# An accumulating gather for the first expert row of each token, in the combine stage of a mixer and mixture-of-experts block

## The chip, the cores and the metric

The kernel runs on one core of a Trainium2 chip. The metric is the device time of one execution in microseconds (us), and lower is better. The engines of the core are named as the profile names them: PE (matrix multiplications; PEld is its weight load), DVE (vector), ACT (scalar, activations), POOL (general purpose, and issuer of indirect DMAs) and SP (issuer of plain DMAs). Each works through its own list in order and is held only by semaphores. Sixteen DMA engines move the data of all DMAs.

## What is computed

One block of a diffusion transformer over 512 tokens of width 1024, in float32: a parallel mixer (short convolution, multiscale pooling, neighbourhood attention, Fourier mix), then a mixture of experts in which each token goes to 2 of 16 experts, then a last norm. The part that the change touches is the end:

```python
def moe_ffn(h, router_w, router_b, w1, w3, w2):
    ...
    _, idx = lax.top_k(masked, TOP_K)                      # two experts for each token
    ...
    for e in range(N_EXPERTS):
        he = jax.nn.silu(h @ w1[e]) * (h @ w3[e])
        y = y + gates[:, e:e + 1] * (he @ w2[e]).astype(F32)
    return y.astype(h.dtype)
...
    f = moe_ffn(tokens, ...)
    x = x + g2 * f[:b * n].reshape(b, n, d)
    ...
return rms_norm(x, final_g)
```

So each output row is the residual row plus two scaled expert rows, divided by its root mean square and multiplied by `final_g`.

## The kernel before, in words

The mixer and the routing come first, then the experts. Each expert has a block of up to 128 token rows (and there are spare blocks for experts that are chosen by more). The blocks run in pairs, one after the other: the matrix products stand on PE, the splits of each float32 weight into a high and a low part on ACT and DVE. A block ends in `ysb`, 128 rows of 1024 values that are already multiplied by gate and `g2`, and ACT stores them in a table in device memory, `expert_rows` (`y_dram` in the code).

The combine stage begins while the last block is still on PE. It works on four chunks of 128 tokens, t = 0 to 3. `x1[:, t, :]` holds the residual rows, `slot_idx[:, t, k]` says in which row of the table the k-th expert row of a token stands, and two banks of PSUM (`tok_bank(t, half)`, 512 columns each) hold the sum of chunk t. The last block of all is not read back from the table: `y_hi` and `y_lo`, its rows split in two, are multiplied by a 0/1 matrix `last_hot` on PE and land in the same banks (`last_to_tokens`). Four steps surround the change:

- POOL (L801 to L808) waits until the rows of all blocks but the last are in the table, and issues eight gathers, two for each chunk, into `ygat[:, t, 0, :]` and `ygat[:, t, 1, :]`. Both gathers of a chunk raise `gat_in[t]` by 16.
- DVE adds, for the chunks 0, 1 and 2, the first gathered row to the residual (`add_first`, L2207, which waits for `gat_in[t]`) and then the second gathered row to that, into PSUM (`add_second`, L2211, which raises `xsum_ok`). Between the ones for chunk 0 and the others stand the scaling of the last block's rows (L2138) and the low half of its split (L2217).
- For chunk 3, ACT copies the residual into PSUM (L1705, raises `x3_ok`), and PE adds both gathered rows by multiplying them with the identity (`gathered_row`, L1325).
- When PE has finished chunk t (`tok_ok`), ACT squares and sums it (L1709) and takes a root (L1712), DVE takes the reciprocal (L2221) and scales both halves (`result`, L2224), and SP stores each half in `out` (L634). Each of these runs over t = 0 to 3 in this order on its engine.

The order on every engine is written out by hand. A semaphore `fresh_ok` says that the PSUM banks of a chunk have been opened by a matrix product (L1290).

Of the kernel before, what the change touches and what calls it, by code (L numbers as in the profile page):

```python
# [30 lines left out]
ALU = mybir.AluOpType  # L31
# [40 lines left out]
def build(nc, x, c, ctx, c_ctx, ada_w, ada_b, norm1_g, norm2_g, w_in, conv_w, pool_w, pool_scale,  # L72
# [3 lines left out]
    y_dram = nc.dram_tensor("expert_rows", ((NB + 1) * P, D), F32, kind="Internal").ap()  # L76
# [4 lines left out]
    with stack:  # L81
        def at(name, offset, shape, dt=F32):
            return nc.alloc_sbuf_tensor_at(name, shape, dt, offset=base + int(offset))

        def sem(name):
            return stack.enter_context(nc.semaphore(name))
# [47 lines left out]
        ygat = at("ygat", 0, [P, NT, 2, D])  # L134
# [7 lines left out]
        x1 = at("x1", 128 * K1, [P, NT, D])  # L142
# [40 lines left out]
        def small(name, shape, dt=F32, pool=1):  # L183
            n = int(np.prod(shape[1:])) * mybir.dt.size(dt)
            n = (n + 31) // 32 * 32
            t = at(name, cursor[pool], shape, dt)
            cursor[pool] += n
            return t

        ident = small("ident", [P, P])  # L190
# [25 lines left out]
        slot_idx = small("slot_idx", [P, NT, 2], I32)  # L216
# [56 lines left out]
        psum = stack.enter_context(nc.psum_tensor("psum", [P, 8, 512], F32))  # L273
# [136 lines left out]
        gat_in = [sem(f"gat_in{i}") for i in range(NT)]  # L410
        xsum_ok = sem("xsum_ok")
        x3_ok = sem("x3_ok")
        fresh_ok = sem("fresh_ok")
        ylast_hi_ok = sem("ylast_hi_ok")
        ylast_lo_ok = sem("ylast_lo_ok")
        tok_ok = sem("tok_ok")
# [38 lines left out]
        def tok_bank(t, half):  # L455

            return bank[2 * t + half]
# [183 lines left out]
        def _(gp):  # L641
# [160 lines left out]
            gp.wait_ge(ysb_free[1], n_pairs * 16)  # L802
            gp.sem_inc(gather_go, 1)
            for t in range(NT):
                for k in range(2):
                    gp.indirect_dma_start(ygat[:, t, k, :], None, y_dram,
                                          bass.IndirectOffsetOnAxis(ap=slot_idx[:, t, k:k + 1], axis=0)
                                          ).then_inc(gat_in[t], 16)  # L808

# [2 lines left out]
        def _(pe):  # L814
# [198 lines left out]
            for h in range(2):  # L1013
                pe.matmul(bank[4 + h][:], pw[:, h, :], dpool[:, h, :],
                          start=True, stop=True).then_inc(pool_ps, 1)

            for t in range(NT):
                for h in range(2):
                    m = pe.matmul(bank[t][:, h * GW:(h + 1) * GW], fT[:, h, t * P:(t + 1) * P], head_dft[:],
                                  start=True, stop=True)  # L1020
# [130 lines left out]
            for i in range(NT):  # L1151
                m = pe.matmul(bank[7][:, NT * NE:(NT + 1) * NE], ones_b[:], sel[:, i, :],
                              start=(i == 0), stop=(i == NT - 1))
# [3 lines left out]
            for i in range(2 * NT):  # L1157
                m = pe.matmul(bank[6][:, 0:2 * NE], hot_slot[:, i, :], hot_base[:, i].rearrange("p a b -> p (a b)"),
                              start=(i == 0), stop=(i == 2 * NT - 1))
# [160 lines left out]
            pe.wait_ge(y1_copied, last + 1)  # L1320
            whole_bank_written(6).then_inc(fresh_ok, 1)

            def gathered_row(half, k):
                hs = slice(half * 512, (half + 1) * 512)
                return pe.matmul(tok_bank(3, half)[:], ident[:], ygat[:, 3, k, hs], start=False, stop=(k == 1))  # L1325

            def last_to_tokens(t, half):
                hs = slice(half * 512, (half + 1) * 512)
                cols_ = last_hot[:, t * P:(t + 1) * P]
                pe.wait_ge(ylast_hi_ok, half + 1)  # L1330
                pe.matmul(tok_bank(t, half)[:], cols_, y_hi[:, hs], start=False, stop=False)
                pe.wait_ge(ylast_lo_ok, half + 1)
                return pe.matmul(tok_bank(t, half)[:], cols_, y_lo[:, hs], start=False, stop=(t < 3))

            pe.wait_ge(xsum_ok, 1)
            last_to_tokens(0, 0)
            last_to_tokens(0, 1).then_inc(tok_ok, 1)
            pe.wait_ge(x3_ok, 1)
            for half in range(2):
                last_to_tokens(3, half)  # L1340
            pe.wait_ge(xsum_ok, 2)
            last_to_tokens(1, 0)
            last_to_tokens(1, 1).then_inc(tok_ok, 1)
            pe.wait_ge(gat_in[3], 32)
            for half in range(2):
                gathered_row(half, 0)
            pe.wait_ge(xsum_ok, 3)
            last_to_tokens(2, 0)
            last_to_tokens(2, 1).then_inc(tok_ok, 1)
            gathered_row(0, 1)  # L1350
            gathered_row(1, 1).then_inc(tok_ok, 1)

# [2 lines left out]
        def _(act):  # L1357
# [342 lines left out]
            for half in range(2):  # L1700
                hs = slice(half * 512, (half + 1) * 512)
                act.wait_ge((y0_copied, y1_copied)[half], last + 1)
                act.copy(y_hi[:, hs], ysb[1][:, hs]).then_inc(ylast_hi_ok, 1)
            act.wait_ge(fresh_ok, 4)
            act.copy(psum[:, 6:8, :].rearrange("p a n -> p (a n)"), x1[:, 3, :]).then_inc(x3_ok, 1)  # L1705

            for t in range(NT):
                act.wait_ge(tok_ok, t + 1)
                act.activation(ygat[:, t, 0, :], psum[:, 2 * t:2 * t + 2, :].rearrange("p a n -> p (a n)"), ACT.Square,  # L1709
                               accum_out=st2[:, t, 6:7]).then_inc(ss3_ok, 1)  # L1710
                act.wait_ge(ss3_ok, t + 1)
                act.activation(st2[:, t, 7:8], st2[:, t, 6:7], ACT.Sqrt, bias=eps[:], scale=1.0 / D  # L1712
                               ).then_inc(root3_ok, 1)

# [2 lines left out]
        def _(v):  # L1719
            step = [0]  # L1720

            def link(ins):

                step[0] += 1
                ins.then_inc(dve_step, 1)
                v.wait_ge(dve_step, step[0])
# [59 lines left out]
            for n in range(4, 10):  # L1786
                a = ADA_SLOT[n]
# [331 lines left out]
            def low_hidden(b, s):  # L2119
                v.wait_ge(het_hi_ok, s + 1)  # L2120
                v.tensor_tensor(heT_lo[b][:].rearrange("p k t -> p (k t)"), bank[4],
                                heT_hi[b][:].rearrange("p k t -> p (k t)"), ALU.subtract).then_inc(het_lo_ok, 1)
# [8 lines left out]
            def expert_rows(b, s, i, half):  # L2131

                v.wait_ge((y0_ok, y1_ok)[half], s + 1)
                if half == 0:
                    v.wait_ge(ysb_free[b], i * 16 + 16)
                    v.wait_ge(gs_ok, s + 1)
                cs_ = slice(half * 512, (half + 1) * 512)
                v.scalar_tensor_tensor(out=ysb[b][:, cs_], in0=bank[5 + half], scalar=gs1[b][:, 0:1],  # L2138
                                       in1=rows[:, G2, cs_], op0=ALU.mult, op1=ALU.mult
                                       ).then_inc((y0_copied, y1_copied)[half], 1)  # L2140
# [61 lines left out]
            final = n_pairs - 1  # L2202
            block_(0, last - 1, last - 2, n_pairs - 2, last - 3)

            def add_first(t):
                v.wait_ge(gat_in[t], 32)
                link(v.tensor_tensor(x1[:, t, :], ygat[:, t, 0, :], x1[:, t, :], ALU.add))  # L2207

            def add_second(t):
                v.wait_ge(fresh_ok, t + 1)  # L2210
                v.tensor_tensor(psum[:, 2 * t:2 * t + 2, :].rearrange("p a n -> p (a n)"), ygat[:, t, 1, :], x1[:, t, :],  # L2211
                                ALU.add).then_inc(xsum_ok, 1)
# [30 lines left out]
            v.tensor_scalar(last_hot[:], iota_tok[:], idx_last[:, 0:1], None, ALU.is_equal).then_inc(hot_ok, 1)  # L2243
            gated(last)
            low_hidden(1, last)
            add_first(0)
            expert_rows(1, last, final, 0)
            add_second(0)
            expert_rows(1, last, None, 1)
            low_last(0)  # L2250
            low_last(1)
            for t in (1, 2):
                add_first(t)
                add_second(t)
            v.wait_ge(gain_in, 48)
            for t in range(NT):
# [45 lines left out]
```

## Time and profile before

| | before |
|---|---|
| median of 3 runs | 601.15 us |
| lowest and highest of these | 600.04 and 601.83 us |
| profiled execution, its own time | 599.58 us |
| its span, first to last instruction | 597.8 us |
| granted TensorE clock, mean over the span | 0.977 of full |

The span is 1.8 us shorter than the time of the same execution. PE is busy for 553.1 us of the span, DVE for 442.8, ACT for 320.3 and POOL for 155.7. These shares are averages over stages with different limits; what is touched here lies in the last 30 us, from the first gather at 569.5 us to the end of the last store.

### The profile page before, as it was taken

Reading aid. Unit: us, or ns where it says so; the run is one execution under the profiler, and the core shown is the slowest. Engines: PE = TensorE matmul, PEld = TensorE weight load, DVE = VectorE, ACT = ScalarE, POOL = GpSimd, SP = SyncE. Lnnn points to the kernel's source line nnn. Section 1 sums busy time; section 2 is a strip of 40 time slices with the busy share of each in tenths; the row PEclk is TensorE's granted clock in tenths of the full one; section 3 lists DMA queues with packets and bytes.
Section 4 is the critical chain, followed back from the end, with each engine's and each line's share of the span. In section 5 each row is a group of like instructions: output and inputs, shape, how many; then the busy total and the mean of one; then the engine's idle time right before and its main releaser. Section 6 shows DMA issues by size and latency. Waiting matters only on the chain.

```text
span 597.8 us, 7516 instructions
## 1 busy us (share of the span) xinstructions
PE 553.1 (93%) x2681; PEld 412.6 (69%) x2681; DVE 442.8 (74%) x569; ACT 320.3 (54%) x394; POOL 155.7 (26%) x139
## 2 busy tenths in 40 slices
PE   1789998999999999985998999999999999999995
PEld 1345873677676787752577887888888888778772
DVE  1358693545586545428769999999999999999868
ACT  4530133345424922235438766768766768766624
POOL 5000916333220700023243113333112333110060
PEclk9789999999999999987999999999999999999998
DMA  8999997369223720058769999999999999999665
GB/s 309 389 371 321 379 369 254 101 191 357 72 70 128 247 84 36 35 210 303 241 227 390 365 398 391 392 392 392 389 392 391 390 392 390 370 383 369 209 213 210
DMA packets 89323, 172.05 MB, mean 288 GB/s; under 512 B 5514, under 2 KB 19022, under 8 KB 89298
## 3 DMA queue, kind: packets, MB, share of 16 engines
q1 hardware_dynamic: 83010, 153.34, 71.7%
q10 hardware_dynamic: 2768, 9.97, 4.1%
q0 software_dynamic: 3520, 8.42, 4.0%
q8 instruction: 15, 0.25, 0.2%
q14 instruction: 10, 0.07, 0.0%
HBM read 158.58 MB, written 17.32 MB: 294 GB/s over the span
## 4 chain that ended last, share of the span: by engine, by line
PE 76%; DMA 10%; DVE 5%; SPq 4%; ACT 3%; issue 1%; DVEq 0%; ACTq 0%; POOLq 0%
DMA ada<-in_ada_w 9%; PE psum L1209 5%; PE psum L1210 5%; PE psum L1211 5%; PE psum L1221 5%; PE psum L1220 5%; PE psum L1219 5%; PE psum L1236 4%; PE psum L1238 4%; PE psum L1237 4%; PE psum L934 3%; PE psum L936 3%; PE psum L935 3%; PE psum L1071 2%; PE psum L1183 2%; PE psum L1073 2%
## 5 line engine op out<-in xcount | busy, mean ns | idle before, releaser
L2116 DVE TENSOR_TENSOR w_lo<-w,w_hi 128x2048 fp32r<-128x2048 f32 x32 | 72.9, 2280 | 2.4 <-ACT w_hi L1622 2.4
L2105 DVE TENSOR_TENSOR w_lo<-w,w_hi 128x1024 fp32r<-128x1024 f32 (+2 forms) x30 | 68.7, 2293 | 0.0
L1622 ACT CAST w_hi<-w 128x2048 fp32r<-128x2048 f32 x32 | 60.3, 1918 | 10.7 <-DMA w<-in_moe_w 5.2
L1613 ACT CAST w_hi<-w 128x2048 fp32r<-128x2048 f32 x30 | 57.2, 1910 | 14.8 <-PE psum L1221 10.9
L2099 DVE TENSOR_TENSOR w_lo<-w,w_hi_a 128x2048 fp32r<-128x2048 f32 (+1 forms) x30 | 51.5, 1755 | 3.0 <-ACT w_hi_a L1609 2.7
L763 POOL COPY idx<-idx 128x1 int32 (+1 forms) x14 | 11.7, 833 | 153.0 <-PE psum L1183 152.4
L1236 PE MATMUL psum<-w_hi,heT_hi 128*128 128x512 f32 x120 | 49.7, 414 | 0.7 <-DVE w_lo L2116 0.7
L1238 PE MATMUL psum<-w_hi,heT_lo 128*128 128x512 f32 x120 | 47.0, 392 | 0.0
L1210 PE MATMUL psum<-w_lo,xgT_hi 128*128 128x512 f32 x120 | 46.8, 390 | 0.0
L1237 PE MATMUL psum<-w_lo,heT_hi 128*128 128x512 f32 x120 | 46.7, 389 | 0.0
L1219 PE MATMUL psum<-w_hi,xgT_hi 128*128 128x512 f32 x120 | 46.7, 389 | 0.0
L1220 PE MATMUL psum<-w_lo,xgT_hi 128*128 128x512 f32 x120 | 46.7, 389 | 0.0
L1221 PE MATMUL psum<-w_hi,xgT_lo 128*128 128x512 f32 x120 | 46.7, 389 | 0.0
L1609 ACT CAST w_hi_a<-w 128x1024 fp32r<-128x1024 f32 x45 | 44.2, 1049 | 0.6 <-DMA w<-in_moe_w 0.6
L1791 DVE SCALAR_TENSOR_TENSOR rows<-ada,cc,rows 128x512 f32<-128x512 f32 x48 | 37.9, 792 | 7.6 <-DMA ada<-in_ada_w 6.1
L780 POOL COPY gs<-gslot 128x1 f32 x14 | 34.4, 2457 | 30.1 <-DVE ysb L2138 30.1
L704 POOL TENSOR_TENSOR win_lo<-win,win_hi 128x1024 fp32r<-128x1024 f32 x10 | 23.8, 2385 | 61.8 <-ACT win_hi L1407 61.8
L1645 ACT ACTIVATE sg<-psum 128x512 f32<-128x512 f32 x16 | 9.6, 599 | 56.1 <-PE psum L1211 50.2
L934 PE MATMUL psum<-hT_hi,win_hi 128*128 128x512 f32 x80 | 33.1, 414 | 3.5 <-DVE z L1859 1.5
L1209 PE MATMUL psum<-w_hi_a,xgT_hi 128*128 128x512 f32 x90 | 36.2, 402 | 0.1
L1211 PE MATMUL psum<-w_hi_a,xgT_lo 128*128 128x512 f32 x90 | 35.1, 390 | 0.0
L936 PE MATMUL psum<-hT_hi,win_lo 128*128 128x512 f32 x80 | 31.3, 392 | 0.0
(345 smaller groups left out, 1255.0 us busy)
## 6 DMA issues: line engine op xcount, KB each, us to landing
w<-in_moe_w SPq DMA_DIRECT2D x32, 2048.0 KB, 14.3
w<-in_moe_w SPq DMA_DIRECT2D x32, 1024.0 KB, 14.0
ada<-in_ada_w SPq DMA_DIRECT2D x12, 2048.0 KB, 18.1
win<-in_w_in SPq DMA_DIRECT2D x8, 1024.0 KB, 14.1
expert_rows<-ysb ACTq DMA_DIRECT2D x15, 512.0 KB, 6.3
expert_rows<-zero SPq DMA_DIRECT2D x1, 5120.0 KB, 21.3
wout<-in_w_out SPq DMA_DIRECT2D x4, 1024.0 KB, 4.9
x<-in_x SPq DMA_DIRECT2D x2, 1024.0 KB, 9.9
```

The lines of the kernel that those rows point to most:

```text
L1209: pe.matmul(bank[2][:], xgT_hi[:, k, :], w_hi, start=(k == 0), stop=False)
L1210: pe.matmul(bank[2][:], xgT_hi[:, k, :], w1_lo[b][:, k, :], start=False, stop=False)
L1211: m = pe.matmul(bank[2][:], xgT_lo[:, k, :], w_hi, start=False, stop=(k == KD - 1))
L1219: pe.matmul(bank[3][:], xgT_hi[:, k, :], w3_hi[:, k, :], start=(k == 0), stop=False)
L1220: pe.matmul(bank[3][:], xgT_hi[:, k, :], w3_lo[b][:, k, :], start=False, stop=False)
L1221: m = pe.matmul(bank[3][:], xgT_lo[:, k, :], w3_hi[:, k, :], start=False, stop=(k == KD - 1))
L1236: pe.matmul(bank[5 + half][:], heT_hi[b][:, k, :], w2_hi[:, k, hs], start=(k == 0), stop=False)
L1237: pe.matmul(bank[5 + half][:], heT_hi[b][:, k, :], w2_lo[b][:, k, hs], start=False, stop=False)
L1238: m = pe.matmul(bank[5 + half][:], heT_lo[b][:, k, :], w2_hi[:, k, hs], start=False, stop=(k == KF - 1))
L1622: act.copy(w2_hi[:, :, hs], w2_sb[b][:, :, hs]).then_inc(w2_hi_ok[half], 1)
L2105: v.tensor_tensor(w3_lo[b][:, ks, :], w3_sb[b][:, ks, :], w3_hi[:, ks, :], ALU.subtract).then_inc(w3_lo_ok, n)
L2116: v.tensor_tensor(w2_lo[b][:, :, hs], w2_sb[b][:, :, hs], w2_hi[:, :, hs], ALU.subtract).then_inc(w2_lo_ok[half], 1)
```

## The change

The first gather of each chunk adds its rows to `x1[:, t, :]` while it moves them; the second gather stays as it was. `add_first` goes away on DVE, and `add_second` now waits for `gat_in[t]`. On PE, chunk 3 takes only one gathered row, and it comes after the chunks 1 and 2. On ACT, the copy of `x1[:, 3, :]` into PSUM waits for `gat_in[3]` and stands behind the square and the root of chunk 0.

```diff
@@ gpsimd @@
             for t in range(NT):
-                for k in range(2):
-                    gp.indirect_dma_start(ygat[:, t, k, :], None, y_dram,
-                                          bass.IndirectOffsetOnAxis(ap=slot_idx[:, t, k:k + 1], axis=0)
-                                          ).then_inc(gat_in[t], 16)
+                gp.indirect_dma_start(x1[:, t, :], None, y_dram,
+                                      bass.IndirectOffsetOnAxis(ap=slot_idx[:, t, 0:1], axis=0),
+                                      compute_op=ALU.add).then_inc(gat_in[t], 16)
+                gp.indirect_dma_start(ygat[:, t, 1, :], None, y_dram,
+                                      bass.IndirectOffsetOnAxis(ap=slot_idx[:, t, 1:2], axis=0)
+                                      ).then_inc(gat_in[t], 16)
@@ tensor @@
             last_to_tokens(0, 1).then_inc(tok_ok, 1)
+            pe.wait_ge(xsum_ok, 2)
+            last_to_tokens(1, 0)
+            last_to_tokens(1, 1).then_inc(tok_ok, 1)
+            pe.wait_ge(xsum_ok, 3)
+            last_to_tokens(2, 0)
+            last_to_tokens(2, 1).then_inc(tok_ok, 1)
             pe.wait_ge(x3_ok, 1)
             for half in range(2):
                 last_to_tokens(3, half)
-            pe.wait_ge(xsum_ok, 2)
-            last_to_tokens(1, 0)
-            last_to_tokens(1, 1).then_inc(tok_ok, 1)
-            pe.wait_ge(gat_in[3], 32)
-            for half in range(2):
-                gathered_row(half, 0)
-            pe.wait_ge(xsum_ok, 3)
-            last_to_tokens(2, 0)
-            last_to_tokens(2, 1).then_inc(tok_ok, 1)
-            gathered_row(0, 1)
-            gathered_row(1, 1).then_inc(tok_ok, 1)
+            gathered_row(0)
+            gathered_row(1).then_inc(tok_ok, 1)
@@ scalar @@
-            act.wait_ge(fresh_ok, 4)
-            act.copy(psum[:, 6:8, :].rearrange("p a n -> p (a n)"), x1[:, 3, :]).then_inc(x3_ok, 1)
 
             for t in range(NT):
...
                 act.activation(st2[:, t, 7:8], st2[:, t, 6:7], ACT.Sqrt, bias=eps[:], scale=1.0 / D
                                ).then_inc(root3_ok, 1)
+                if t == 0:
+                    act.wait_ge(gat_in[3], 32)
+                    act.wait_ge(fresh_ok, 4)
+                    act.copy(psum[:, 6:8, :].rearrange("p a n -> p (a n)"), x1[:, 3, :]).then_inc(x3_ok, 1)
@@ vector @@
-            def add_first(t):
+            def add_second(t):
                 v.wait_ge(gat_in[t], 32)
-                link(v.tensor_tensor(x1[:, t, :], ygat[:, t, 0, :], x1[:, t, :], ALU.add))
-
-            def add_second(t):
                 v.wait_ge(fresh_ok, t + 1)
...
-            add_first(0)
             expert_rows(1, last, final, 0)
             add_second(0)
...
             for t in (1, 2):
-                add_first(t)
                 add_second(t)
```

How this moves instructions is shown in two places. On ACT at the end, before (`x_111` is `x1`; `st_173` holds the sums and roots):

```order
L1703 CAST y_hi<-ysb_134 128x512 [waits y1_copied]
L1705 COPY psum<-x_111 128x1024 [waits fresh_ok]
L1709 ACTIVATE ygat,st_173<-psum 128x1024 [waits tok_ok]
L1712 ACTIVATE st_173<-st_173,eps 128x1 [waits ss3_ok]
```

and after, the same place:

```order
L1702 CAST y_hi<-ysb_134 128x512 [waits y1_copied]
L1706 ACTIVATE ygat,st_173<-psum 128x1024 [waits tok_ok]
L1709 ACTIVATE st_173<-st_173,eps 128x1 [waits ss3_ok]
L1714 COPY psum<-x_111 128x1024 [waits fresh_ok,gat_in3]
```

The copy of the residual of chunk 3 went behind the square and root of chunk 0, and got a second semaphore to wait for; the squares and roots of the chunks 1, 2 and 3 stand behind it, as they did.

On DVE from the low part of the last hidden rows to the first result, before:

```order
L2121 TENSOR_TENSOR heT_lo_150<-psum,heT_hi_148 128x512 [waits het_hi_ok]
L2207 TENSOR_TENSOR x_111<-ygat,x_111 128x1024 [waits gat_in0]
L2138 SCALAR_TENSOR_TENSOR ysb_134<-psum,gs_1_158,rows 128x512 [waits ysb_free1,gs_ok,y0_ok,dve_step]
L2211 TENSOR_TENSOR psum<-ygat,x_111 128x1024 [waits fresh_ok]
L2138 SCALAR_TENSOR_TENSOR ysb_134<-psum,gs_1_158,rows 128x512 [waits y1_ok]
L2217 TENSOR_TENSOR y_lo<-ysb_134,y_hi 128x512 [waits ylast_hi_ok] x2
L2207 TENSOR_TENSOR x_111<-ygat,x_111 128x1024 [waits gat_in1]
L2211 TENSOR_TENSOR psum<-ygat,x_111 128x1024 [waits fresh_ok,dve_step]
L2207 TENSOR_TENSOR x_111<-ygat,x_111 128x1024 [waits gat_in2]
L2221 RECIPROCAL st_173<-st_173 128x1 [waits root3_ok,gain_in]
```

and after:

```order
L2122 TENSOR_TENSOR heT_lo_150<-psum,heT_hi_148 128x512 [waits het_hi_ok]
L2139 SCALAR_TENSOR_TENSOR ysb_134<-psum,gs_1_158,rows 128x512 [waits gs_ok,ysb_free1,y0_ok]
L2209 TENSOR_TENSOR psum<-ygat,x_111 128x1024 [waits fresh_ok,gat_in0]
L2139 SCALAR_TENSOR_TENSOR ysb_134<-psum,gs_1_158,rows 128x512 [waits y1_ok]
L2215 TENSOR_TENSOR y_lo<-ysb_134,y_hi 128x512 [waits ylast_hi_ok] x2
L2209 TENSOR_TENSOR psum<-ygat,x_111 128x1024 [waits fresh_ok,gat_in1]
L2209 TENSOR_TENSOR psum<-ygat,x_111 128x1024 [waits fresh_ok,gat_in2]
L2219 RECIPROCAL st_173<-st_173 128x1 [waits root3_ok,gain_in]
```

Three additions of 128x1024 are gone, and the waits for the gathers moved from the first addition of a chunk to the second.

## Rows read from the trace of the kernel before

**Rows 1.** The head of the page: span, busy time and share of each engine, instructions.

```profile
span 597.8 us, 7516 instructions
PE 553.1 (93%) x2681; PEld 412.6 (69%) x2681; DVE 442.8 (74%) x569; ACT 320.3 (54%) x394; POOL 155.7 (26%) x139
```

**Rows 2.** DVE in order of time: start, us, engine, line, operation, idle before and releaser.

```profile
577.75 1.23 DVE L2207 TENSOR_TENSOR x<-ygat,x 128x1024 f32<-128x1024 f32 x1 [1.03 <-DMA ygat<-expert_rows,slot_idx]
...
579.85 1.22 DVE L2211 TENSOR_TENSOR psum<-ygat,x 128x1024 f32<-128x1024 f32 x1
582.07 0.75 DVE L2138 SCALAR_TENSOR_TENSOR ysb<-psum,gs,rows 128x512 f32<-128x512 f32 x1 [1.00 <-PE psum L1310]
582.74 1.46 DVE L2217 TENSOR_TENSOR y_lo<-ysb,y_hi 128x512 fp32r<-128x512 f32 x2
584.12 1.22 DVE L2207 TENSOR_TENSOR x<-ygat,x 128x1024 f32<-128x1024 f32 x1
...
588.91 0.15 DVE L2221 RECIPROCAL st<-st 128x1 f32<-128x1 f32 x1
...
593.72 0.16 DVE L2221 RECIPROCAL st<-st 128x1 f32<-128x1 f32 x1
593.92 1.41 DVE L2224 SCALAR_TENSOR_TENSOR ygat<-psum,st,fing 128x512 f32<-128x512 f32 x2
```

**Rows 3.** ACT in order of time, the same columns, from the copy for chunk 3.

```profile
583.42 1.02 ACT L1705 COPY psum<-x 128x1024 f32<-128x1024 f32 x1
584.79 1.03 ACT L1709 ACTIVATE ygat<-psum 128x1024 f32<-128x1024 f32 x1 [0.36 <-PE psum L1333]
...
585.94 0.30 ACT L1712 ACTIVATE st<-st,eps 128x1 f32<-128x1 f32 x1
587.88 1.02 ACT L1709 ACTIVATE ygat<-psum 128x1024 f32<-128x1024 f32 x1 [1.65 <-PE psum L1333]
...
592.25 1.02 ACT L1709 ACTIVATE ygat<-psum 128x1024 f32<-128x1024 f32 x1 [0.27 <-PE psum L1325]
...
593.40 0.29 ACT L1712 ACTIVATE st<-st,eps 128x1 f32<-128x1 f32 x1
```

**Rows 4.** POOL in order of time: first, second, sixth and last of the eight gathers.

```profile
569.51 2.85 POOL L806 DMA_INDIRECT ygat<-expert_rows,slot_idx  x1 [5.73 <-DMA expert_rows<-ysb]
572.66 0.94 POOL L806 DMA_INDIRECT ygat<-expert_rows,slot_idx  x1 [0.30 <-issue]
...
577.65 0.94 POOL L806 DMA_INDIRECT ygat<-expert_rows,slot_idx  x1 [0.30 <-issue]
...
580.13 1.74 POOL L806 DMA_INDIRECT ygat<-expert_rows,slot_idx  x1 [0.30 <-issue]
```

**Rows 5.** DMA issues one by one (issue to landing, us): second, fourth and eighth gather.

```profile
ygat<-expert_rows,slot_idx POOLq DMA_INDIRECT x1, 5.1
...
ygat<-expert_rows,slot_idx POOLq DMA_INDIRECT x1, 6.0
...
ygat<-expert_rows,slot_idx POOLq DMA_INDIRECT x1, 6.1
```

**Rows 6.** Stretches of the end: busy us of five engines, PE clock, DMA share, GB/s.

```profile
573.00:576.00 3.00, 2.73 (x14) 1.69 (x12) 0.69 (x1) 0.58 (x1) 2.39 (x3) 1.00 0.87 262
576.00:580.00 4.00, 3.95 (x17) 3.28 (x18) 2.74 (x4) 0.04 (x2) 2.91 (x4) 1.00 0.96 320
582.00:585.00 3.00, 2.33 (x9) 1.24 (x8) 2.84 (x4) 1.79 (x3) 0.00 (x0) 1.00 1.00 410
...
590.00:597.00 7.00, 2.21 (x7) 0.81 (x5) 5.12 (x10) 2.82 (x6) 0.00 (x0) 0.83 0.80 300
```

**Rows 7.** PE in order of time: chunk 1 from its sum, the identity products of chunk 3.

```profile
586.66 0.50 PE L1331 MATMUL psum<-y_hi,last_hot 128*128 128x512 f32 x1 [0.96 <-DVE psum L2211]
...
587.68 1.88 PE L1325 MATMUL psum<-ygat,ident 128*128 128x512 f32 x4
...
590.33 1.88 PE L1325 MATMUL psum<-ygat,ident 128*128 128x512 f32 x4
```

More of the change, by code:

```diff
@@ L1321, in _, with gathered_row @@
             whole_bank_written(6).then_inc(fresh_ok, 1)
-            def gathered_row(half, k):
+            def gathered_row(half):
                 hs = slice(half * 512, (half + 1) * 512)
-                return pe.matmul(tok_bank(3, half)[:], ident[:], ygat[:, 3, k, hs], start=False, stop=(k == 1))
+                return pe.matmul(tok_bank(3, half)[:], ident[:], ygat[:, 3, 1, hs], start=False, stop=True)
             def last_to_tokens(t, half):
```

## The prediction

> **What bounds the kernel now.** I read the page first, then the end of the trace engine by engine. Over the whole span PE is the busiest engine [rows 1], but the change touches only the last 30 us, so only the waits there matter.
>
> The vector engine in order of time [rows 2]: from 582.07 us, where it takes the last expert rows from PE, to 595.33 us (593.92 + 1.41), where the last scaled rows are written, none of its rows carries a wait. First come the scaling and the low part of the last block (to 584.2), then four additions of 128x1024 at 1.22 us each (584.12 to 588.9), then four results, of which the first starts at 588.91 and the last at 593.72. So DVE sets the end, and after its last result 597.8 - 595.33 = 2.47 us go to the last store. Ahead of 582.07 it waits 1.00 us for PE: nothing that is saved on DVE before that point moves the end.
>
> ACT is second [rows 3]. Its copy for chunk 3 runs at 583.42, ahead of the square of chunk 0 (584.79), whose PE work is not ready earlier; the root of chunk 0 ends at 586.24. A square, its read of the sum and a root take 592.25 to 593.69 = 1.44 us for one chunk. Before the square of chunk 1 ACT waits 1.65 us, since PE gets the sum of chunk 1 from DVE only at 586.6 [rows 3, 7].
>
> The gathers: POOL issues the first at 569.51 and the last at 580.13, one each 1.25 us after the second [rows 4]. From issue to landing they take 5 to 6 us [rows 5], so the pair of chunk 0 is in at 572.66 + 5.1 = 577.76 (where DVE's only wait for them ends [rows 2]), that of chunk 1 at 575.16 + 6.0 = 581.2, and the last at 580.13 + 6.1 = 586.23. The third pair is in near 583.75 (issued at 577.65, and landing like the last). The DMA engines are nearly full while they move them: a share of 0.87 at 262 GB/s, then 0.96 at 320, then 1.00 at 410 [rows 6]. A gather is 128 x 4 KB = 524 KB; at 410 GB/s that is 1.28 us of all engines.
>
> **The change part by part.**
>
> *Removed on DVE.* Three additions. The one for chunk 0 lies ahead of the wait that ends at 582.07 and is worth nothing. Those for chunks 1 and 2 go: DVE would do `add_second(1)` at 584.15 to 585.4 and `add_second(2)` to 586.6, 2.4 us earlier than now, if the gathers are in.
>
> *What is late next.* ACT now copies chunk 3 behind the root of chunk 0 (586.24), takes 1.02 us for it [rows 3], and only then squares chunks 1, 2 and 3. Call L the landing of the last gather, and L' the later of L and 586.3. The root of chunk 1 ends at L' + 1.05 + 1.44 = L' + 2.5. DVE's three results behind it then set the pace at 1.55 us each (588.91 to 593.72 is 4.81 for three, with a last wait of 0.1 [rows 2]): the last ends at L' + 2.5 + 3 x 1.55 + 0.1 = L' + 7.25, and the span at L' + 7.25 + 2.47 = L' + 9.75. Against 597.8 the difference is **L' - 588.05**. With L' = 586.3 that is -1.75 us: the whole gain of the change if the gathers are as fast as now. PE has time: after the copy it needs 1.2 us for chunk 3 and half of the 1.88 us of identity products [rows 7], while ACT squares two other chunks for 2.9 us.
>
> *Moved on PE.* Two identity products fewer (0.94 us [rows 7]), and chunks 1 and 2 no longer stand behind chunk 3. PE waits for DVE there (0.96 us [rows 7]), so this costs nothing and is worth nothing beyond what is counted.
>
> *The added wait.* ACT waits for both gathers of chunk 3 before the copy. Queued behind it on ACT are the squares of chunks 1 and 2, which need nothing from chunk 3; behind these wait DVE's results 1 to 3 and six of the eight stores. Before, a late last gather held only PE's products for chunk 3, which begin at 587.68 [rows 7], 1.4 us after the landing. Now each us that L lies beyond 586.3 moves the end by one.
>
> *The accumulating gather.* No row shows one. It has to fetch the 4 KB row of the residual from SBUF besides the row of the table, and write the sum. From below its extra cost c per gather is 0: the same bytes from the table, the same bytes to SBUF. The nearest row for fetching rows out of SBUF is the output stores: 590 to 597 us, a share of 0.80 at 300 GB/s [rows 6], which is 1.40 us of all engines for 524 KB. As a bound from above I take a gather and a full store and a gather in sequence, c = 1.28 + 1.40 = 2.7. Between the ends I take the cost of one more fetch of the same bytes, c = 1.3, since the DMA engines are already full with one fetch and one write for each row, and the write does not double.
>
> The Trainium skill, "Collectives: The Full Stack", section "The bandwidth ceiling", speaks against this change: an add inside a DMA is slow because it needs two source reads on the same ring, and reduce-scatter ran at 32.35 GB/s where all-gather ran at 62.28. No run here shows it yet; by that ratio an accumulating gather would cost 1.28 x 1.93 = 2.47 us, c = 1.2 (an estimate from that page), and the sum would come out 0.4 us lower than mine.
>
> With c = 1.3, four of them add 5.2 us to a queue that is full, less what stands free now between 573 and 580: 3 x 0.13 + 4 x 0.04 = 0.55 us. L = 586.23 + 5.2 - 0.55 = 590.9. Difference: 590.9 - 588.05 = **+2.85 us**.
>
> The other pairs: chunk 0 is in at 577.76 + 1.3 = 579.1, before DVE wants it at 579.93. Chunk 1 at 581.2 + 2.6 - 0.4 = 583.4, before 584.15. Chunk 2 at 583.75 + 3.9 - 0.55 = 587.1: DVE waits 1.7 us for it, `add_second(2)` ends at 588.3, result 0 runs 588.3 to 589.9. All of that is over before ACT's first root behind the copy (593.4), so it costs nothing of its own. Result 0 is stored from 589.2 on, against the last gather, which can cost that up to 1.4 us; I leave it out of the sum and put it in the range.
>
> *POOL.* Its instruction for a plain gather takes 0.94 us and a gap of 0.30 [rows 4]. If one that accumulates takes up to twice as long (1.88), a pair is issued in 3.4 us, while its bytes take 1.28 + 2.58 = 3.9 us of the DMA engines: hidden. Only the first would shift the start, by up to 0.94 us. From below, nothing.
>
> **Sum.** 599.58 + 2.85 = 602.4 us for an execution like the profiled one. That one lies 1.57 us under the median of the runs shown, so for a median I add the same difference to 601.15: **604.0 us**. A difference of 0.3%, 1.8 us, is about what the measurement can tell from none.
>
> **The rivals.**
>
> *A, the forecast:* the second fetch costs a second pass of the DMA engines, the last pair comes 4 to 5 us later, and ACT's new wait passes that on. 604.0. For it: the share of 1.00 while the last gathers move [rows 6], and the place of the wait ahead of the squares. Chance 0.42, with c from 1.0 to 1.8 (602.8 to 606).
>
> *B, the add rides for free* (c under 0.15): the read of the residual hides beside the fetch from device memory. Then L' is 586.3, two additions leave the chain that sets the end, and the time is 601.15 - 1.75 = 599.4. For it: in 573 to 576 the engines move only 262 GB/s at a share of 0.87, against 410 later, so part of their time is waiting and not moving [rows 6]. Against it: at 1.00 and 410 there is nothing left to wait. The sum changes sign at L = 588.05, which is c = (588.05 - 586.23 + 0.55) / 4 = 0.6. Chance 0.17.
>
> *C, part of the cost hides:* c between 0.15 and 1.0, L up to 589.7, time 599.9 to 602.8, 601.2 at c = 0.6. Such would be the case if POOL's issue and not the bytes set the pace. Chance 0.20.
>
> *D, the add is dearer than a fetch:* each row goes as fetch, fetch and write in sequence, c = 1.8 to 2.7 and over. At 2.7, L = 586.23 + 10.8 - 0.55 = 596.5, and the difference is +8.4: 609.6. For it: nothing in the trace; against it: nothing either. Chance 0.21, of which a quarter lies above 2.7.
>
> **How the numbers follow.** The time is that of A. Below, the range reaches to B with 0.4 us for the spread of the median: 599.0. Above it reaches to c = 2.7 without the last few tenths, 609.4; what is left out is near 0.05 above and 0.07 below, and more than that I can't cut without leaving D out. A's own range, with the stores' 1.4 us, is 602.5 to 606.5. Slower by over 0.3% needs c above 1.05: nearly all of A (0.39) and D (0.21), 0.60. Within 0.3%: C, the rest of A and a part of B, whose 1.75 us stand just at the bound: 0.28. Faster by over 0.3%: 0.12.
>
> **What would show it.** Right: POOL's eight gathers land 4 to 5 us later in the end; the DMA share stays at 0.9 or more from 573 to about 590 with fewer GB/s of table rows; ACT stands idle from 586.2 to about 591 ahead of its copy, released by a DMA; its squares of chunks 1 and 2 follow back to back; DVE's four additions are two. Wrong: the last gather lands at 586 to 587 (B), or much beyond 593 (D), or DVE waits at `add_second(0)` beyond 580.9, from which it would hold the last expert rows at 582.07. The place of the wait would be wrong as a cause if ACT's wait is long and yet the results of chunks 1 and 2 come before it ends.

## The result: the changed kernel is slower by 0.9%

| | before | changed |
|---|---|---|
| median | 601.58 us (12 runs) | 606.36 us (12 runs) |
| lowest and highest | 600.04 and 604.01 us | 603.96 and 610.15 us |
| ratio to before, 95% interval | | 1.0089 (1.0073 to 1.0105) |
| profiled execution, its span | 597.8 us | 604.4 us |

The forecast was 604.0 us, with a range of 599.0 to 609.4 and "slower" as the likeliest sign. The sign and the range held, the size did not: a rise of about 2.9 us was forecast and one of 4.8 to 5.4 came. In the two profiled executions it is 6.6 us.

The work ahead of the gathers varies by a few us from one execution to the next: the first gather starts at 569.51 us in the trace of before, at 569.63 in that of the changed kernel, and between 569.8 and 572.3 in those below. So wherever traces are compared from here on, times count from the start of the first gather, called g. A landing is the start of POOL's instruction plus the time from issue to landing. Before: last landing g + 16.7, last result written g + 25.8, end of the span g + 28.3. Changed: g + 22.7, g + 32.3 and g + 34.8.

POOL of the changed kernel in order of time (start, us, engine, line, operation, idle before and what ended it), which answers to [rows 4]:

```profile
569.63 3.62 POOL L805 DMA_INDIRECT x<-expert_rows,slot_idx  x1 [5.60 <-DMA expert_rows<-ysb]
573.56 1.00 POOL L808 DMA_INDIRECT ygat<-expert_rows,slot_idx  x1 [0.30 <-issue]
574.86 1.55 POOL L805 DMA_INDIRECT x<-expert_rows,slot_idx  x1 [0.31 <-issue]
...
582.99 0.98 POOL L808 DMA_INDIRECT ygat<-expert_rows,slot_idx  x1 [0.30 <-issue]
```

An accumulating gather takes POOL 1.55 us instead of 0.94, and the first one 3.62 instead of 2.85. From issue to landing, the sixth and the last of the eight (the second gathers of chunks 2 and 3), against 6.1 us before [rows 5]:

```profile
ygat<-expert_rows,slot_idx POOLq DMA_INDIRECT x1, 8.7
...
ygat<-expert_rows,slot_idx POOLq DMA_INDIRECT x1, 9.3
```

The stretches of the end (busy us of PE, PEld, DVE, ACT and POOL, then the granted PE clock, the DMA share and GB/s), which answer to [rows 6]:

```profile
576.00:580.00 4.00, 3.79 (x17) 3.08 (x17) 1.33 (x2) 0.25 (x1) 3.09 (x4) 1.00 1.01 237
...
582.00:585.00 3.00, 2.38 (x8) 0.85 (x6) 2.28 (x4) 0.62 (x1) 1.66 (x2) 1.00 1.05 259
...
588.00:591.00 3.00, 1.11 (x3) 0.92 (x4) 2.36 (x4) 0.00 (x0) 0.00 (x0) 0.56 0.96 273
591.00:594.00 3.00, 1.61 (x5) 0.80 (x4) 0.35 (x1) 1.72 (x2) 0.00 (x0) 0.50 0.50 187
594.00:597.00 3.00, 3.00 (x7) 1.68 (x6) 2.23 (x5) 1.93 (x6) 0.00 (x0) 0.50 0.16 61
```

In 576 to 580 and in 582 to 585 us the DMA engines are as full as before but move 237 and 259 GB/s where they moved 320 and 410. And there is something that the forecast does not have: the granted clock of PE falls in its wait ahead of chunk 2 and is 0.50 from 588.5 us on, the lower of its two levels, 1.2 of 2.4 GHz. The waits of the changed kernel from 569 us on (who waited for whom, us in total, times, longest):

```profile
DVE st L2219 <- ACT st L1709: 5.8, 2, 3.4
ACT psum L1714 <- DMA ygat<-expert_rows,slot_idx: 5.8, 1, 5.8
...
PE psum L1333 <- DVE psum L2209: 3.7, 2, 2.6
...
ACT ygat L1706 <- PE psum L1327: 2.8, 1, 2.8
DVE psum L2209 <- DMA ygat<-expert_rows,slot_idx: 2.9, 2, 2.6
```

ACT waits 5.8 us for the last gather ahead of its copy, as foreseen. But it also waits 2.8 us ahead of its last square, for PE, and that decides what comes after. PE and ACT at that place, in order of time, which answer to [rows 7] and [rows 3]:

```profile
593.35 0.80 PE L1333 MATMUL psum<-y_hi,last_hot 128*128 128x512 f32 x1 [1.39 <-ACT psum L1714]
593.95 0.63 PE L1335 MATMUL psum<-y_lo,last_hot 128*128 128x512 f32 x1
...
595.23 3.56 PE L1327 MATMUL psum<-ygat,ident 128*128 128x512 f32 x4
```

```profile
592.28 1.02 ACT L1714 COPY psum<-x 128x1024 f32<-128x1024 f32 x1 [5.81 <-DMA ygat<-expert_rows,slot_idx]
593.24 1.02 ACT L1706 ACTIVATE ygat<-psum 128x1024 f32<-128x1024 f32 x1
...
595.70 0.29 ACT L1709 ACTIVATE st<-st,eps 128x1 f32<-128x1 f32 x1
598.83 1.02 ACT L1706 ACTIVATE ygat<-psum 128x1024 f32<-128x1024 f32 x1 [2.83 <-PE psum L1327]
```

ACT is through with chunks 1 and 2 at 596.0. PE needs 593.35 to 598.8 for chunk 3, 5.4 us. The identity products show as four rows for two products, and they take 3.56 us here; the same four rows took 1.88 us at a clock of 1.00 [rows 7].

### The profile page after: what moved, and what is told of

It is laid out like the page before. It is cut to its first block, busy times and chain, and to the rows that moved or that the text cites. A ratio compares the mean times of both kernels' runs of the same rounds, so it can differ in the third digit from the quotient of the medians.

```text
span 604.4 us, 7506 instructions
## 1 busy us (share of the span) xinstructions
PE 553.4 (92%) x2677; PEld 413.4 (68%) x2677; DVE 444.1 (73%) x566; ACT 320.0 (53%) x394; POOL 158.6 (26%) x139
## 4 chain that ended last, share of the span: by engine, by line
PE 69%; DMA 12%; SPq 7%; DVE 4%; ACT 3%; issue 2%; POOL 2%; POOLq 0%; DVEq 0%; ACTq 0%
DMA ada<-in_ada_w 6%; PE psum L1238 4%; PE psum L1211 4%; PE psum L1240 4%; PE psum L1212 4%; PE psum L1213 4%; PE psum L1239 4%; PE psum L1223 4%; PE psum L1221 4%; PE psum L1222 4%; DMA w<-in_moe_w 3%; PE psum L936 3%; PE psum L938 3%; SPq L510 3%; PE psum L937 3%; PE psum L1073 2%
## 5 line engine op out<-in xcount | busy, mean ns | idle before, releaser
L1792 DVE SCALAR_TENSOR_TENSOR rows<-ada,cc,rows 128x512 f32<-128x512 f32 x48 | 41.4, 866 | 9.6 <-DMA ada<-in_ada_w 8.1
```

## Experiments

Two theories were to be told apart. The forecast's: the late last gather is passed on by ACT's queue, with the squares of chunks 1 and 2 behind the copy. The other, from the trace of after: PE, slowed by its clock, sets the end after the copy.

### The wait out of the way of the squares

```diff
-                if t == 0:
+                if t == 2:
                     act.wait_ge(gat_in[3], 32)
```

> The changed kernel with one edit: the scalar engine's copy of chunk 3 and its wait for the last gather stand behind the square and root of chunk 2, no longer behind those of chunk 0. Theory 1 (the forecast's: the new wait is dear because the squares of chunks 1 and 2 and the results behind them are queued behind it): these are out of the way before the last landing (592.3 us), and the end comes 2 us or more earlier than in the changed kernel, near 602.4 us of span instead of 604.4. Theory 2 (what sets the end is TensorE, which after the copy needs 5.5 us for chunk 3, 593.4 to 598.8, at a granted clock of 0.50, while the scalar engine is through at 596.0 and waits 2.8 us): the copy stays at 592.3, TensorE still ends near 598.8, and the span stays within 0.4 us of 604.4.

Measured: 607.22 us, 1.0092 (1.0062 to 1.0122) of before. The last gather lands at g + 22.1, the last result is written at g + 32.8 (the changed kernel: 32.3). The results of chunks 1 and 2 do come early, and it does not help (vector engine, then ACT and PE, in order of time):

```profile
593.06 0.15 DVE L2219 RECIPROCAL st<-st 128x1 f32<-128x1 f32 x1
...
595.27 0.16 DVE L2219 RECIPROCAL st<-st 128x1 f32<-128x1 f32 x1 [0.61 <-ACT st L1709]
...
603.20 0.16 DVE L2219 RECIPROCAL st<-st 128x1 f32<-128x1 f32 x1 [6.32 <-ACT st L1709]
```

```profile
595.14 1.00 ACT L1714 COPY psum<-x 128x1024 f32<-128x1024 f32 x1
601.73 1.02 ACT L1706 ACTIVATE ygat<-psum 128x1024 f32<-128x1024 f32 x1 [5.58 <-PE psum L1327]
```

```profile
598.07 3.62 PE L1327 MATMUL psum<-ygat,ident 128*128 128x512 f32 x4
```

The last reciprocal waits 6.32 us instead of 2.48: what was queued before is now idle time. ACT's place for the wait is not what costs here; the chain from the landing through the copy, PE, the last square and the last result is. The copy even starts a little late here (g + 23.1), behind the root of chunk 2. The forecast's theory falls in this step, though at a low clock: in this trace PE's clock has fallen to 0.50 already at g + 16.0, when chunk 1 begins. How the two chains compare at full clock is seen in the next run.

### PE kept at work while it waits

```diff
-            whole_bank_written(6).then_inc(fresh_ok, 1)
+            def filler():
+                pe.matmul(bank[6][:], last_hot[:, 0:P], last_hot[:], start=True, stop=True)
...
+            for _ in range(4):
+                filler()
             pe.wait_ge(xsum_ok, 2)
...
+            for _ in range(11):
+                filler()
+            whole_bank_written(6).then_inc(fresh_ok, 1)
             pe.wait_ge(xsum_ok, 3)
```

> The changed kernel with 4 products of 128x512 ahead of chunk 1 and 11 ahead of chunk 2 on TensorE, into a bank that is written anew afterwards; they only keep TensorE at work while it waits for the late gathers. Theory 2 (clock): the granted clock stays near 1.0 to about 592 us and does not stand at 0.50 in 593 to 597, the four products of chunk 3 and its identity products take 3.1 us instead of 5.5, and the span is 2.0 to 2.4 us shorter than the changed kernel's 604.4, near 602.2. If the clock of 0.50 comes from something else than the idle time (the DMA traffic or the stores), it falls all the same and the span stays at 604.4; if the fillers hold up the chunks, it grows.

Measured: 606.11 us, 1.0087 (1.0059 to 1.0115), from four runs, so the time alone tells nothing. The profile does. Clock and DMA in the same stretches, and the identity products:

```profile
588.00:591.00 3.00, 3.00 (x15) 2.35 (x14) 1.95 (x3) 0.00 (x0) 0.00 (x0) 1.00 1.04 255
591.00:594.00 3.00, 0.49 (x3) 0.05 (x1) 0.76 (x2) 0.69 (x1) 0.00 (x0) 1.00 0.71 272
594.00:597.00 3.00, 2.62 (x8) 1.43 (x8) 1.24 (x3) 2.93 (x7) 0.00 (x0) 1.00 0.00 0
```

```profile
595.41 1.88 PE L1329 MATMUL psum<-ygat,ident 128*128 128x512 f32 x4
```

The clock stays at 1.00, the identity products take 1.88 us again, and chunk 3 is done in 2.95 us (594.38 to 597.33). The last result is written at g + 30.0, 2.3 us before the changed kernel's, although the last gather lands at g + 22.9. The DMA engines are as full as in the changed kernel (a share of 1.04 against 0.96 in 588 to 591), so it is PE's idle time that goes with the fall of the clock: in the changed kernel PE is busy for 1.11 of 3 us in 588 to 591, here for 3.00. At what point the clock falls these rows do not settle: in the two traces of the changed kernel it falls in the wait ahead of chunk 2, in that of `e1_copy_late` already where chunk 1 begins, after a wait of 0.65 us.

At full clock the two chains end together (ACT, then the vector engine, in order of time):

```profile
597.33 1.02 ACT L1713 ACTIVATE ygat<-psum 128x1024 f32<-128x1024 f32 x1 [0.31 <-PE psum L1329]
...
598.47 0.29 ACT L1716 ACTIVATE st<-st,eps 128x1 f32<-128x1 f32 x1
```

```profile
597.44 1.41 DVE L2229 SCALAR_TENSOR_TENSOR ygat<-psum,st,fing 128x512 f32<-128x512 f32 x2
598.80 0.17 DVE L2226 RECIPROCAL st<-st 128x1 f32<-128x1 f32 x1
```

ACT waits 0.31 us for PE ahead of its last square, and its last root ends at 598.76; the vector engine is through with the third result at 598.85 and takes the last reciprocal without a wait. So here, too, moving the wait alone could gain at most 0.1 us; no run has both edits.

Because four runs were too few, both kernels ran again side by side.

> The changed kernel itself, timed beside the other kernels of this series. Measured first: 1.0089 of the kernel before. It should come out at 1.007 to 1.011 again, with the last gather 22.6 us after the start of the first, and TensorE at a granted clock of 0.50 from 591 to 597 us.

Measured: 605.86 us, 1.0094 (1.0062 to 1.0126). Its trace repeats the first in its main points: last landing g + 22.7, last result g + 32.3, and

```profile
591.00:594.00 3.00, 1.98 (x4) 1.16 (x4) 2.44 (x4) 0.00 (x0) 0.00 (x0) 0.50 0.75 252
594.00:597.00 3.00, 1.38 (x4) 1.09 (x4) 0.00 (x0) 2.32 (x5) 0.00 (x0) 0.50 0.40 147
```

> The changed kernel with 15 filler products on TensorE once more. Its profiled execution was 2.3 us shorter than the changed kernel's from the first gather to the end (32.5 against 34.8 us), its four timed runs were not shorter. If the fall of the clock is a part of the cost in most executions, it comes out 0.2 to 0.4% under the changed kernel, 1.005 to 1.007. If the clock is a part of the cost only in the execution that was profiled, both come out alike.

Measured: 605.31 us, 1.0069 (1.0043 to 1.0096), clock 1.00 to 597 us, last landing g + 22.0, last result g + 29.2. The mean clock of the span is 0.977 to 0.981 in all six timed runs and 0.968 to 0.974 in the seven of the changed kernel, which speaks for a fall of the clock in the usual execution too; in the earlier runs the two overlap (0.976 to 0.980 in four, 0.970 to 0.978 in twelve). In the traces the last result comes 2.3 and 3.1 us earlier, of which 0.7 us in the second are an earlier landing: from the landing to the last result there are 7.1 and 7.2 us where the changed kernel needs 9.6. In the medians of this series the difference is 0.5 us, in its means 1.7 us (605.1 against 606.8), and over both series, 10 runs against 19, 1.3 us of mean, though these were not all run side by side. The intervals of the two kernels overlap. That the clock is part of the cost is shown by the traces; that it is worth all of 2.4 us in the timed runs is not. In the second trace the stores behind the last result also took 3.9 us instead of 2.5, which takes back part of it there; why is open.

### The same kernel with plain gathers

```diff
                 gp.indirect_dma_start(x1[:, t, :], None, y_dram,
-                                      bass.IndirectOffsetOnAxis(ap=slot_idx[:, t, 0:1], axis=0),
-                                      compute_op=ALU.add).then_inc(gat_in[t], 16)
+                                      bass.IndirectOffsetOnAxis(ap=slot_idx[:, t, 0:1], axis=0)).then_inc(gat_in[t], 16)
```

> The changed kernel with the first gather of each chunk plain: it overwrites the residual instead of adding to it, so the residual is left out of the output. Everything else, and the order of it, is as in the changed kernel. Both theories: POOL's instructions fall from 1.55 to 0.94 us, the first from 3.62 to 2.85; the last gather lands at 586.2 us instead of 592.3; the clock does not fall before 592; the end is L' + 9.75 with L' = 586.3, 596.05 us of span, 1.75 us under the kernel before. If the two additions less on the vector engine are worth nothing, the span is 597.8 as before.

Measured: 599.27 us, 0.9976 (0.9960 to 0.9992) of before. The last gather lands at g + 16.5, the last result is written at g + 23.8, 2.0 us before that of the kernel before, and the end comes at g + 26.3. POOL's instructions are the old ones:

```profile
570.13 2.74 POOL L805 DMA_INDIRECT x<-expert_rows,slot_idx  x1 [5.83 <-DMA expert_rows<-ysb]
...
580.64 1.67 POOL L807 DMA_INDIRECT ygat<-expert_rows,slot_idx  x1 [0.31 <-issue]
```

This is the rest of the change without its one dear part: fewer additions on the vector engine and fewer products are worth 0.24% (0.08 to 0.40), which is 1.4 us, where the forecast had worked out 1.75. All of the loss, and more, comes with the accumulation.

### Two accumulating gathers

```diff
-                                      compute_op=ALU.add).then_inc(gat_in[t], 16)
+                                      **(dict(compute_op=ALU.add) if t < 2 else {})).then_inc(gat_in[t], 16)
```

> The changed kernel with only the first gathers of chunks 0 and 1 accumulating; those of chunks 2 and 3 are plain and overwrite the residual, which is left out for these chunks. The theory that each accumulating gather costs the queue the same: from the start of the first gather to the last landing it takes 22.6 us with four and 16.8 with none, so 19.7 us with two; the span from the first gather to the end is near 29.5 us (26.3 with none, 34.8 with four, since the clock need not fall with the shorter wait). If the cost is mostly a single one (the first accumulating instruction on POOL), the last landing comes at 21 us or later.

Measured: 602.75 us, 1.0026 (1.0003 to 1.0049). Last landing g + 19.3, end g + 29.4, where 19.7 and 29.5 were expected. With none, two and four the landing comes at 16.5, 19.3 and 22.7: 1.4 us for each of the first two and 1.7 for each of the others, near to a line. So it is not one single cost at the start. The clock did fall here, against the expectation, but it came back in the stage, at g + 21.5, so that chunk 3 has its identity products at full clock again:

```profile
588.00:591.00 3.00, 2.51 (x5) 1.60 (x6) 1.68 (x4) 1.52 (x2) 0.00 (x0) 0.55 0.50 191
591.00:594.00 3.00, 2.98 (x8) 1.40 (x7) 2.03 (x5) 2.13 (x6) 0.00 (x0) 0.88 0.20 77
```

### Half the bytes, the same number of instructions and rows

```diff
-                gp.indirect_dma_start(x1[:, t, :], None, y_dram,
+                gp.indirect_dma_start(x1[:, t, 0:512], None, y_dram.rearrange("r (h d) -> (r h) d", h=2),
```

> The changed kernel with the accumulating gathers of half width: 512 columns instead of 1024, from a table seen as rows of 512, so other rows are read and the right half of the first expert row is left out. The number of instructions and of rows is the same. If bytes decide (a second fetch of the same bytes), an accumulating gather costs half of its 2.5 us on the DMA engines, and the last landing comes 4 to 5 us earlier, at 17.5 to 18.5 us after the start of the first gather instead of 22.6. If POOL's instruction (1.55 us and a gap of 0.30) or the number of rows decides, the last landing stays at 21 us or more.

Measured: 601.54 us, 1.0011 (0.9993 to 1.0029). The last landing comes at g + 19.2, 3.5 us earlier than with full rows, and less than the 4 to 5 us that bytes alone would give. POOL explains the difference, as far as these rows show. It issues the last gather at g + 13.3 here as in the changed kernel, and that gather lands 5.9 us later, about as in the kernel before (6.1 us in [rows 5]); with full rows it is 9.3 us. So with full rows the bytes decide, and close behind them stands POOL, whose issuing is 2.7 us longer than before (g + 13.36 against g + 10.62 for the last).

### The accumulating gathers alone

```diff
-                gp.indirect_dma_start(ygat[:, t, 1, :], None, y_dram,
-                                      bass.IndirectOffsetOnAxis(ap=slot_idx[:, t, 1:2], axis=0)
-                                      ).then_inc(gat_in[t], 16)
...
-                v.wait_ge(gat_in[t], 32)
+                v.wait_ge(gat_in[t], 16)
```

> The changed kernel without its four plain gathers: only the accumulating ones are left, and where the second rows were read, the residual rows are read instead, so the second expert row of each token is left out. It measures the accumulating gather by itself. If it needs 2.5 us of the DMA engines, more than the 1.85 us in which POOL issues one (1.55 and a gap of 0.30), the landings stand 2.3 to 2.6 us apart and the last comes about 15 us after the start of the first. If the engines take one in less than 1.85 us, they stand 1.85 apart, the latency stays the same from the first to the last, and the last comes at 13 to 14 us.

Measured, in a single run: 600.53 us beside a median of 600.88 for the kernel before. The four land at g + 8.2, 11.0, 15.0 and 17.4, 2.8, 4.0 and 2.4 us apart, 3.1 us on average; POOL issues them 1.85 us apart. So the engines need more than POOL, as the first branch said, but the last lands 2.4 us later than it said. In the stretches where only these gathers move:

```profile
577.00:583.00 6.00, 5.78 (x27) 4.51 (x26) 2.52 (x3) 1.21 (x2) 3.09 (x2) 1.00 1.05 193
```

At a full share of the engines they move 193 GB/s of table rows, against 410 for plain gathers [rows 6]: 2.1 times the price. The Trainium skill, "Collectives: The Full Stack", section "The bandwidth ceiling", gives a measured ratio of 1.93 between all-gather and reduce-scatter, whose add reads two sources; the ratio in these traces is a tenth above that.

### A version with two accumulating gathers in better places

The kernel before, with only the first gathers of chunks 3 and 2 accumulating, issued fifth and sixth, and the copy of chunk 3 left ahead of the squares:

```diff
-            for t in range(NT):
-                for k in range(2):
-                    gp.indirect_dma_start(ygat[:, t, k, :], None, y_dram,
...
+            for t, k in ((0, 0), (0, 1), (1, 0), (1, 1), (3, 0), (2, 0), (2, 1), (3, 1)):
+                if t >= 2 and k == 0:
+                    gp.indirect_dma_start(x1[:, t, :], None, y_dram,
+                                          bass.IndirectOffsetOnAxis(ap=slot_idx[:, t, 0:1], axis=0),
+                                          compute_op=ALU.add).then_inc(gat_in[2] if t == 2 else table_in, 16)
+                else:
...
```

> The kernel before with only two of its four first gathers accumulating, those of chunks 3 and 2, issued fifth and sixth, each before the plain second gather of its chunk. The first addition of chunk 2 on the vector engine and two of the four identity products of chunk 3 on TensorE go; the copy of chunk 3 stays ahead of the square of chunk 0 and waits for its own gather. With 1.2 to 1.6 us more for each accumulating gather: the chunks 0 and 1 as before, the gather of chunk 3 in at 584, the pair of chunk 2 at 586.5, when the vector engine wants it, and the last at 588.7 to 589.0, when TensorE is through with chunk 2. The clock does not fall. The vector engine begins its results 1.2 us earlier and TensorE ends chunk 3 1.2 us earlier: span 596.5, 1.3 us or 0.2% under the kernel before. If the engines' queue delays these gathers as much as four do, the last comes at 592 and the span is 600 or more.

Measured: 601.66 us, 1.0008 (0.9988 to 1.0028): no difference that can be told, instead of 0.2% faster. The pair of chunk 2 lands at g + 18.4, not at the g + 17 that was expected, and the vector engine waits for it:

```profile
590.73 1.23 DVE L2214 TENSOR_TENSOR psum<-ygat,x 128x1024 f32<-128x1024 f32 x1 [1.39 <-DMA ygat<-expert_rows,slot_idx]
```

These 1.39 us are the 1.2 that the addition less had saved.

### The addition on POOL instead of in the DMA

The kernel before, with the first addition of chunk 1 moved from the vector engine to POOL, behind its eight plain gathers:

```diff
+            gp.wait_ge(gat_in[1], 32)
+            gp.tensor_tensor(x1[:, 1, :], ygat[:, 1, 0, :], x1[:, 1, :], ALU.add).then_inc(iota_ok, 1)
...
-            for t in (1, 2):
-                add_first(t)
-                add_second(t)
+            v.wait_ge(iota_ok, 3)
+            add_second(1)
+            add_first(2)
+            add_second(2)
```

> The kernel before with the first addition of chunk 1 on POOL instead of the vector engine, behind the eight plain gathers, which stay as they are. It tests whether the gain of a shorter vector engine can be had without a dearer DMA. POOL is free at 12.4 us after the first gather starts and chunk 1 is in at 11.6. A POOL addition of 128x512 took 1.28 us in the kernel before, so 2.6 us for 128x1024: done at 15.0, when the vector engine wants it at 14.6. Then the results begin 0.8 us earlier, TensorE follows, and the span is 0.8 us or 0.1% shorter. If POOL is held up while the vector engine works (copies of 128x1 on POOL took 2.46 us on average in the loop and 0.18 in rest), the addition takes 4 us or more and the span is longer by 1 us or more.

Measured: 601.57 us, 1.0013 (0.9995 to 1.0031). The addition on POOL takes 2.4 us where 2.6 were expected, and the last landing stays at g + 16.7. But the vector engine pays for it (POOL, then the vector engine):

```profile
582.81 2.37 POOL L810 TENSOR_TENSOR x<-ygat,x 128x1024 f32<-128x1024 f32 x1
```

```profile
583.34 3.00 DVE L2219 TENSOR_TENSOR y_lo<-ysb,y_hi 128x512 fp32r<-128x512 f32 x2
```

The two subtractions that take 1.46 us beside an idle POOL [rows 2] take 3.00 us while POOL adds (582.81 to 585.18). These 1.5 us more are what the addition less (1.22 us) had saved, and the last result comes at g + 26.0, after g + 25.8 before. Neither version beats the kernel before.

## Why the prediction was wrong in size, step by step

- *What bounds the kernel now* held: the plain variant gained 1.4 us (0.24%, 0.5 to 2.4 us) where 1.75 were worked out from the two additions on DVE.
- *The accumulating gather*, c = 1.3 us over a plain one, held nearly: from the pair of chunk 1 to that of chunk 3 the landings of a pair stand 3.75 us apart, where pairs of plain ones stood 2.55 apart; counted over the whole series, four accumulating gathers against none move the last landing by 22.7 - 16.5 = 6.2 us, 1.55 each, with the longer first instruction in it.
- *L* was mis-sized by 1.3 us (g + 22.7 against 590.9 - 569.5 = g + 21.4). Two items of its sum failed. I took off 0.55 us for time of the engines that stands free between 573 and 580; it was not filled: from 573 to 576 us the share is 0.70 in the changed kernel, less than the 0.87 of before [rows 6], and the sign that it stays at 0.9 or more from 573 us on did not come. And I called POOL hidden, but its first accumulating instruction is 0.77 us longer and shifts all that follows; I had named this and left it out of the sum. Together these are the 1.3 us. The stores of result 0, for which the forecast kept up to 1.4 us in its range, are issued from 590.7 us on, ahead of the landing; no run separates them from the two items.
- *"PE has time"* is the step that failed. It held two errors. The four rows of the identity products are two products, not four, so the change takes 1.88 us of them away, not 0.94, and leaves chunk 3 with a full 1.88 us and not half of it. At full clock PE has no time to spare then, and ACT waits 0.31 us for it, but that costs the sum nothing (chunk 3 took 2.95 us with the fillers, and the last result came 7.1 us after the landing, against 7.25 forecast). The other is the clock: the late gathers leave PE idle for 2.6 us ahead of chunk 2 and 1.4 us ahead of chunk 3, its clock falls to 0.50, and chunk 3 takes 5.4 us. That is the missing 2.4 us: from the landing of the last gather to the last result there are 9.6 us where 7.25 were forecast.
- *The place of ACT's wait* was right as a wait (5.8 us) and wrong as a cause. With the squares moved out from behind it, nothing was gained, because the chain from the copy through PE is the longer one. The sign that the forecast named for this, results of chunks 1 and 2 ahead of the end of ACT's wait, could not show in the changed kernel, where they are queued behind it; it took the experiment. At full clock both chains end within 0.1 us, so the forecast's 7.25 us came out right there by a path that PE shares.
- The sum over again for the profiled execution: 2.85 forecast, 1.3 for L, 2.4 for the clock, 6.55 us; 6.6 was measured. The medians show 4.8 to 5.4, less than the two traces; why is open. The clock can come back within the stage, as in the trace with two accumulating gathers, but where it did so in the timed runs was not recorded.

## What to carry to other kernels

In this kernel an add that is folded into a DMA is paid by the DMA engines: they are full while the gathers run, and it costs about one more transfer of the same bytes, here 1.55 us each to save additions of 1.22 us on an engine, one of them hidden anyway. Before moving work onto a transfer that is waited for at the end, price the wait of every engine behind it, TensorE's clock among them: here an engine left idle by late transfers came back at half speed for the work that stands last.

## What the runs showed of the hardware that I had not expected

- PE's granted clock fell from 1.00 to 0.50 in the wait of 2.6 us ahead of chunk 2 (0.56 on average in 588 to 591) and was still at 0.50 while PE was busy for all of 594 to 597 us; with filler products in the gaps ahead of chunks 1 and 2 it stayed at 1.00. With two accumulating gathers it fell too, and was back at 1.00 from g + 21.5 on.
- An accumulating gather of 128 rows of 4 KB took POOL 1.55 us and a plain one 0.94; alone, four of them moved 193 GB/s at a full DMA share.
- A POOL addition held up work of the vector engine: its 1.46 us of subtractions took 3.00 us beside a POOL addition of 2.37 us.
